# Four weight panels of a state-space stage multiplied raw in fp32, and a sum of squares placed one panel later

## The reference

```
u = h @ w_in                      # z, xbc, dt, q, k, v, gate logits
xbc = silu(conv(xbc))             # xs, bm, cm
y = ssd(xs, dt_f) + flipped ssd(xs, dt_b) + d_skip * xs
y = y * silu(z)
yg = y in 4 groups of 512 columns
yg = yg * rsqrt(mean(yg**2) + eps) * ssd_norm_w
mix = (gate0 * (yg @ w_proj_ssd) + gate1 * (attention @ w_proj_attn)) @ w_out
```

## Time and profile before

| | |
|---|---|
| median of 3 runs | 1236.75 us |
| profiled execution | 1237.23 us |
| its span | 1235.4 us |
| TensorE busy | 1167.6 us (95%) |
| VectorE busy | 911.1 us (74%) |
| ScalarE busy | 616.7 us (50%) |
| loop of the state-space stage | about 848 to 925 us of the span |
| sums of squares | 935.8 to 951.4 us |

### The profile page before, as it was taken

One profiled execution on the slowest core, in us unless ns is written; L12 is line 12 of the kernel. 1 busy time (PEld: TensorE's weight loads), 2 busy tenths in 40 slices (PEclk: granted clock), 3 DMA queues, 4 the chain that ended last, 5 costly groups with the idle time before them and its releaser, 6 DMA issues.

```text
span 1235.4 us, 19788 instructions
## 1 busy us (share of the span) xinstructions
PE 1167.6 (95%) x8054; PEld 1062.1 (86%) x8054; DVE 911.1 (74%) x1205; ACT 616.7 (50%) x815; POOL 58.0 (5%) x61
## 2 busy tenths in 40 slices
PE   2999999999999999999999999999898998999996
PEld 2978989999988888999999989988787997888885
DVE  6879798887778977765567469886994748656555
ACT  3753354444465435444444335558896733444441
POOL 1016000000000510000000000000000000000000
PEclk8899999999999999999999999999998999999998
DMA  9835468778765416555566534455772564455540
GB/s 381 357 154 205 172 238 290 290 251 307 263 228 225 171 63 223 178 198 174 200 240 199 197 122 136 143 204 168 255 267 79 199 220 161 170 177 198 191 149 34
DMA packets 44059, 249.35 MB, mean 202 GB/s; under 512 B 4352, under 2 KB 12672, under 8 KB 15952
## 3 DMA queue, kind: packets, MB, share of 16 engines
q1 hardware_dynamic: 43568, 246.19, 55.8%
q0 software_dynamic: 416, 2.11, 0.4%
HBM read 247.17 MB, written 1.11 MB: 201 GB/s over the span
## 4 chain that ended last, share of the span: by engine, by line
PE 82%; DVE 8%; ACT 5%; DMA 2%; issue 1%; SPq 0%; POOL 0%; DVEq 0%; ACTq 0%; POOLq 0%
PE bank L428 17%; PE bank L429 16%; PE bank L430 16%; PE bank L785 14%; PE bank L788 7%; PE bank L868 2%; DMA raw<-in_panels 2%; PE bank L909 1%; DVE ring_w L423 1%; ACT mixf L1931 1%; PE bank L1703 1%; PE bank L1821 1%; PE bank L1755 1%; PE bank L767 1%; ACT mixf L1932 1%
## 5 line engine op out<-in xcount | busy, mean ns | idle before, releaser
L423 DVE TENSOR_TENSOR ring_w<-raw,w_hi 128x2048 fp32r<-128x2048 f32 x170 | 390.7, 2300 | 143.6 <-ACT w_hi L418 143.1
L418 ACT ACTIVATE w_hi<-raw 128x2048 fp32r<-128x2048 f32 x170 | 324.2, 1910 | 169.4 <-PE bank L430 156.3
L428 PE MATMUL bank<-act,w_hi 128*128 128x256 f32 x792 | 231.0, 292 | 4.1 <-DVE act L1186 2.7
L429 PE MATMUL bank<-act,w_hi 128*128 128x256 f32 x792 | 225.7, 285 | 0.0
L430 PE MATMUL bank<-act,ring_w 128*128 128x256 f32 x792 | 225.6, 285 | 0.0
L785 PE MATMUL bank<-act,w_hi 128*128 128x512 f32 x736 | 185.7, 394 | 0.2 <-DVE act L2258 0.2
L428 PEld LDWEIGHTS bank<-act,w_hi 128*128 128x128 f32 x792 | 153.6, 194 | 12.3 <-issue 11.9
L429 PE MATMUL bank<-ff_lo,w_hi 128*128 128x256 f32 (+1 forms) x560 | 158.2, 283 | 0.0
L430 PE MATMUL bank<-ff_hi,ring_w 128*128 128x256 f32 (+1 forms) x560 | 158.2, 283 | 0.0
L428 PE MATMUL bank<-ff_hi,w_hi 128*128 128x256 f32 (+1 forms) x560 | 157.7, 282 | 0.0
L785 PEld LDWEIGHTS bank<-act,w_hi 128*128 128x128 f32 x736 | 134.3, 190 | 25.4 <-issue 0.6
(11 more groups left out here) (345 smaller groups left out, 1837.1 us busy)
## 6 DMA issues: line engine op xcount, KB each, us to landing
raw<-in_panels SPq DMA_DIRECT2D x170, 1024.0 KB, 4.8
arena<-in_modw SPq DMA_DIRECT2D x44, 1024.0 KB, 7.0
mixf<-dscr SPq DMA_DIRECT2D x8, 512.0 KB, 4.7
arena<-dscr SPq DMA_DIRECT2D x8, 512.0 KB, 5.0
mixf<-in_modw SPq DMA_DIRECT2D x2, 1024.0 KB, 16.2
act_flat<-in_modw SPq DMA_DIRECT2D x2, 1024.0 KB, 19.9
mixf<-dscr SPq DMA_DIRECT2D x8, 256.0 KB, 5.8
arena<-dscr SPq DMA_DIRECT2D x8, 256.0 KB, 6.5
```

What stands on the lines that cost most here:

```text
L418: nc.scalar.activation(w_hi[slot(k)][:, :], w_raw(m, k), ACT.Copy).then_inc(hi_done, 1)
L423: nc.vector.tensor_tensor(w_lo(m, k), w_raw(m, k), w_hi[slot(k)][:, :].bitcast(F32), ALU.subtract).then_inc(lo_done, 1)
L428: nc.tensor.matmul(o, wh, xh, start=start, stop=False, skip_group_check=skip)
L429: nc.tensor.matmul(o, wh, xl, start=False, stop=False, skip_group_check=skip)
```

## The change

Panels 26, 28, 30 and 32 are no longer split. TensorE waits until such a panel has landed and multiplies it raw in fp32 with the unsplit `x`: 16 products instead of 48. `split_hi` and `split_lo` skip it, and the waits on `hi_done` and `lo_done` count without it (`rounded`). Apart from that, the sums of squares of parts 0 and 1 follow panel 34 instead of 33 and those of parts 2 and 3 panel 35 instead of 34; on ScalarE the roots and the first splits of the result move one gate panel later too.

```diff
+WHOLE = (26, 28, 30, 32)
...
+        def whole(m, k):
+
+            return not isinstance(m, Turn) and 4 * m + k - L_PANELS * layers in WHOLE
+
+        def rounded(m, k):
+
+            c = (m.c if isinstance(m, Turn) else m) * 4 + k - L_PANELS * layers
+            return 4 * m + k + 1 - sum(w < c for w in WHOLE)
...
         def split_hi(act, m, k):
 
+            if whole(m, k):
+                return
             landed(act, m, k)
...
         def split_lo(dve, m, k):
 
-            dve.wait_ge(hi_done, 4 * m + k + 1)
+            if whole(m, k):
+                return
+            dve.wait_ge(hi_done, rounded(m, k))
...
             def panel2(k, arr=None):
                 free2(pe, k)
+                if whole(M2, k):
+                    landed(pe, M2, k)
+                    for n in range(16):
+                        c, kc = n // KC, n % KC
+                        w = w_raw(M2, k)[:, kc * 256 + c * P:kc * 256 + (c + 1) * P]
+                        last = nc.tensor.matmul(G2(k)[:, c * T:(c + 1) * T], w, x[:, kc, :], start=kc == 0, stop=kc == KC - 1)
+                    pe_used(pe, last)
+                    return
...
             for i in range(4):
                 panel2(K_LATE + i)
-                for n in ((0, 1), (2, 3), (), ())[i]:
+                for n in ((), (0, 1), (2, 3), ())[i]:
...
                 split_hi(act, M2, K_LATE + 4 + i)
-                if i == 1:
+                if i == 2:
...
-                if i in (1, 2):
-                    n = i - 1
+                if i in (2, 3):
+                    n = i - 2
```

More of the change, by code:

```diff
@@ L478, in pe_panel @@
         def pe_panel(pe, m, k, o, xh, xl, arrive=None, steps=(0, 16)):
-            pe.wait_ge(lo_done, 4 * m + k + 1)
+            pe.wait_ge(lo_done, rounded(m, k))
             wh, wl = w_hi[slot(k)], w_lo(m, k)
@@ L504, in pe_head_late @@
         def pe_head_late(pe, m, k, o, arrive):
-            pe.wait_ge(hi_done, 4 * m + k + 1)
+            pe.wait_ge(hi_done, rounded(m, k))
             wh, wl = w_hi[slot(k)], w_lo(m, k)
@@ L759, in up_head @@
             def up_head(mm, k, jn):
-                pe.wait_ge(lo_done, 4 * mm + k + 1)
+                pe.wait_ge(lo_done, rounded(mm, k))
                 wh, wl = w_hi[slot(k)], w_lo(mm, k)
@@ L1650, in pe_second @@
                 free2(pe, k)
-                pe.wait_ge(lo_done, 4 * M2 + k + 1)
+                pe.wait_ge(lo_done, rounded(M2, k))
                 for tt in range(TT):
```

## The result

The changed kernel took 1229.85 us (median of 5 runs, 1229.29 to 1230.79), the kernel before 1236.75 (5 runs as well, 1235.01 to 1241.09): ratio 0.9938, 95% interval 0.9920 to 0.9956. So it is faster by less than 1%: 5.4 to 9.9 us in the first timing, 3.1 to 5.8 in the second. The forecast was 1232.5, 4.3 us faster: right sign and mechanism, 2.65 us too slow beside the first median. The first ratio applied to the 1236.75 of before gives 1229.1, just under the lower end of the forecast's range, 1229.5. In the profile of the changed kernel the span went from 1235.4 to 1228.1 us, by 7.3.

A forecast was written before the change was run, and what follows sets the result against it. A ring of ScalarE's decays and VectorE's weighting and masks was taken to pace the even rounds, not TensorE. Reorder -5.9 plus clock 1.6 gave -4.3 us: 1237.23 - 4.3 = 1232.9, stated as 1232.5, range 1229.5 to 1235.8.

The forecast's parts named there:

- The raw panel: TensorE, state-space loop: a raw panel takes 6.9 us, 1.0 longer (0.7 to 1.4), at no cost on the path.
- steps 5, 9 and 13: Steps of the weighted sums in the state-space loop: TensorE's idle time ahead of them falls under 1 us.
- The roundings: Roundings of the raw panels dropped on ScalarE (1.9 us each) and VectorE (2.3 us each): all eight priced at 0.
- The bound of 2 us: Upper bound on the gain from dropped roundings: TensorE's remaining idle time, about 0.6 to 0.8 us in three pairs.
- The reorder: Behind the loop, sums one panel later: panel 37 starts 5.9 us earlier, with a 2.5 us wait ahead of panel 34.
- 0.6 us of cover: Panel 41: VectorE has it rounded at 981.5 us, TensorE wants it at 982.1, so the order holds.
- The slower rival: Raw panels in the loop: the clock falls, a panel takes about 13.4 us, total 1252 us; chance 0.08.
- the clock term: Half clock behind the new 2.5 us wait ahead of panel 34: costs 1.6 us, bounds 0 and 3.1.
- the row nearest in length: The profiled 1.82 us wait ahead of step 13, followed by half speed, with 1.6 us lost.
- hu 6: One of eight state-space loop rounds, hu 0 to 7; each multiplies panel 25+hu, then does steps 2hu and 2hu+1.
- The base of the sum: One profiled execution of the kernel before, 1237.23 us, 0.5 above the median 1236.75, from which 4.3 was subtracted.

The follow-up runs named there:

- raw_only: Changed kernel with the sums of squares and roots back in the old order, panels 26, 28, 30 and 32 still raw: 1236.53 us, ratio 0.9999.
- reorder_only: Changed kernel with no raw panels, only the sums of squares one panel later: 1229.54 us, ratio 0.9943 to the kernel before.
- after: The changed kernel itself, first timing and profile: 1229.85 us, ratio 0.9938 to the kernel before.
- after_again: The changed kernel unedited, timed and profiled again (the second timing): 1230.72 us, ratio 0.9964 to the kernel before.
- raw_even_rounds: Changed kernel with panels 25, 27, 29 and 31 raw instead of 26, 28, 30 and 32: 1231.39 us, ratio 0.9954 to the kernel before.
- raw_conv: Changed kernel with six more raw panels (12, 14, 16, 18, 20, 22) in the convolution stage: 1236.99 us, ratio 1.0007 to the kernel before.
- early_no_raw: Changed kernel with ScalarE's eviction of panel 32 ahead of the silus and no raw panels, run twice: 1226.86 and 1227.02 us, ratios 0.9943 and 0.9920.
- gate_late: Changed kernel with ScalarE's eviction of panel 32 moved behind the rounding of panel 36: 1234.21 us, ratio 0.9990 to the kernel before.

## Why the prediction was right and where it was wrong

- **The raw panel**, 6.9 us forecast, was 7.01, 32 passes of 0.219 us. The idle times ahead of steps 5, 9 and 13 are 0.42, 0.67 and 0.66, under 1 as forecast, and step 13 kept its place to 0.03 us. The Trainium skill, "TensorE: Matmul & The Clock Gate", section "LDWEIGHTS", gives the estimate of 107 ns for a load of 128 columns; with one ahead of each pass, by the prediction's sum, the panel would have taken 10.3 us. The measured 7.01 doesn't bear that out: the loads lie beside the passes.
- **The roundings**, priced at 0: right, by raw_only and by the idle times that grew by as much on ScalarE. The bound of 2 us was never drawn on.
- **The reorder**, -5.9 us with a wait of 2.5: -5.8 with a wait of 2.32, ended by the named eviction. reorder_only shows that it is the whole gain. It is 2.5 of wait and 3.1 of clock. Panel 41, with its 0.6 us of cover, was not waited for.
- **The slower rival**, a clock that falls over the fp32 work: the clock was 1.00 over all four raw panels and what lies between them, so it didn't happen.
- **The step that failed is the clock term**: "I take 1.6, of the row nearest in length". In the profile of the changed kernel the price was 0, and the stretch moved by the bare -5.8. The error was not the bounds (0 to 3.1) but taking the term for a size. It is a draw: of five profiles with a wait of 2.32 to 2.35 us the clock held in two (after, reorder_only) and fell in three (after_again, raw_even_rounds, raw_conv), and a fall cost 1.3 to 1.5 us. The row that I took my value from, step 13 of hu 6, was one draw too: there the same wait, of 1.81 and 1.82 us, was followed by full clock in reorder_only and both runs of early_no_raw, whose eight passes took 1.08 us. And its 1.6 us were TensorE's alone. Panel 33 came only 0.28 us later for it (67.44 against 67.16 in reorder_only). Behind the new wait nothing else waits, and there a fall costs its full price. In the stretch, -4.3 is what the kernel does when the clock falls, -5.8 when it holds. As ratios these are 0.9965 and 0.9953: the second timing, 0.9964, lies between them, the first, 0.9938, beyond both.
- **The base of the sum** was the other error. I had subtracted the gain from the time of one execution of the kernel before, and the two profiles differ by 7.3 - 5.8 = 1.5 us outside the stretch: 1.76 ahead of it, in the draws shown above, less 0.27 behind it. By medians the two timings are 0.9944 (1229.85 of 1236.75) and 0.9956 (1230.72 of 1236.21), closer than 0.9938 and 0.9964; single long executions, such as 1241.09 of before and 1236.96 of after_again, spread them. How often the clock falls behind this wait of 2.3 us stays open: five profiles are too few, and the timed runs show no clock behind it. Two other waits of like length, in the last section, were followed by half clock in 9 and in 7 of 13 profiles.

## What to carry to other kernels

Ask of each part of a change which wait it shortens: here the part with many edits (raw panels) moved work under existing waits and was worth nothing, while four changed lines in two queues were worth 5.8 us, because they put a panel between a result and its reader, and the wait that was left didn't always cost the clock. When a wait goes, look at who releases the next one: the 2.3 us left over was one eviction queued behind work that nobody waited for, and moving that line gained another 2.6 us of the stretch. Price the clock behind an idle time as two cases with a chance each, and compare kernels over the stretch that the change touches before comparing spans.

## What the hardware showed that I had not expected

TensorE's clock after an idle time of a given length differs between executions of one program. After 2.32 us (after) panel 34 took 5.86 us, after 2.34 us (after_again) 7.35. Idle times of 4.14, 4.82 and 5.09 us were followed by half clock in the one profile that each was seen in, that of 1.81 to 1.82 us ahead of step 13 in one of four (before; not reorder_only, early_no_raw and early_no_raw_2). Three waits that all thirteen profiles share say more. Behind the 2.69 us near 354 us (360 in gate_late) the clock fell in 7 of 13. Behind the 1.98 to 1.99 us for L2296 (L2274 before) it fell in 9 of 13, and that cost 1.6: from this wait to the transposes at L1833 (L1811 before) it is 1034.73 - 1011.26 = 23.47 us in after, where it fell, and 1040.70 - 1018.83 = 21.87 in before, where it held. Behind the 2.99 us that follow there it fell in all thirteen. The Trainium skill, "TensorE: Matmul & The Clock Gate", section "What's actually happening", says that the chip looks at activity on a schedule that the kernel doesn't start, so that the moment of a change of clock differs from run to run; these pairs agree with that, and the schedule itself was not measured here.
